# Reordering the head loop of a hybrid decoder kernel: output maps, state products and memory chunks at other places

## The reference, cut to what matters

```python
_, _, h_r, h_i = lax.associative_scan(_cplx_combine, (a_r, a_i, bu_r, bu_i), axis=1)   # 16 groups of 64 states
y = (jnp.einsum('bsgp,gcp->bsgc', h_r, c_re) - jnp.einsum('bsgp,gcp->bsgc', h_i, c_im) + d * ug)
...
s = (jnp.einsum('bqhd,bkhd->bhqk', qn, k_nope) + jnp.einsum('bqhr,bkr->bhqk', qr, k_rope)) * scale
p = softmax32(jnp.where(kpos[None, :] <= t[:, None], s, NEG_INF))                      # 6 heads, and twice 6 of the sparse group
...
kv = (rmsnorm(mem, g_mem) @ wkv).reshape(bsz, m, 2, XATTN_HEADS, XATTN_DIM)            # keys of the memory: four chunks
```

## Time and profile before

| | |
|---|---|
| median of 3 runs | 1681.85 us (1680.43 to 1685.18) |
| profiled execution | 1679.73 us, span 1677.9 us, clock 0.991 |
| VectorE busy | 1338.6 us (80%) |
| ScalarE busy | 1091.2 us (65%) |
| GpSimd busy | 229.7 us (14%) |

### The profile page before, as it was taken

One profiled execution on the slowest core, in us unless ns is written; L12 is line 12 of the kernel. 1 busy time (PEld: TensorE's weight loads), 2 busy tenths in 40 slices (PEclk: granted clock), 3 DMA queues, 4 the chain that ended last, 5 costly groups with the idle time before them and its releaser, 6 DMA issues.

```text
span 1677.9 us, 24224 instructions
## 1 busy us (share of the span) xinstructions
PE 1632.3 (97%) x8466; PEld 1371.8 (82%) x8466; DVE 1338.6 (80%) x1471; ACT 1091.2 (65%) x1231; POOL 229.7 (14%) x240
## 2 busy tenths in 40 slices
PE   8899999999998999999999999999999999999997
PEld 8788888888897888778888888888888888888785
DVE  7986666555668765688988988988989889889897
ACT  7545444445555554467777777777777777777775
POOL 7751001006414300320000000000000000000200
PEclk9999999999999999999999999999999999999998
DMA  9413437755430253399999999999999999999994
GB/s 392 185 51 126 157 120 312 275 179 195 168 138 30 82 181 111 138 411 377 365 379 388 372 382 375 387 380 374 381 369 383 386 375 362 385 375 362 411 384 168
DMA packets 68357, 476.95 MB, mean 284 GB/s; under 512 B 8027, under 2 KB 8161, under 8 KB 13508
## 3 DMA queue, kind: packets, MB, share of 16 engines
q1 hardware_dynamic: 62188, 451.43, 70.2%
q0 software_dynamic: 5584, 22.97, 3.5%
q10 hardware_dynamic: 520, 1.69, 0.3%
HBM read 463.98 MB, written 13.25 MB: 284 GB/s over the span
## 4 chain that ended last, share of the span: by engine, by line
PE 76%; DVE 9%; issue 8%; ACT 3%; POOL 2%; DMA 1%; DVEq 0%; POOLq 0%; SPq 0%; ACTq 0%
PE bank L480 23%; PE bank L482 23%; PE bank L481 23%; DVE lower L504 2%; PE bank L692 1%; DVE lp L2081 1%; ACT upper L523 1%; ACT upper L500 1%; DVE xel L1096 1%; DMA ring<-in_weights 1%; PE bank L1689 1%; DVE row L2081 1%; POOL lp L2555 1%; POOL lp L1250 1%; POOL small L2555 0%
## 5 line engine op out<-in xcount | busy, mean ns | idle before, releaser
L529 DVE TENSOR_TENSOR lower<-ring,upper 128x2048 fp32r<-128x2048 f32 x368 | 847.0, 2302 | 145.3 <-ACT upper L523 132.2
L523 ACT ACTIVATE upper<-ring 128x2048 fp32r<-128x2048 f32 x369 | 706.6, 1915 | 116.7 <-PE bank L482 104.6
L480 PE MATMUL bank<-upper,xeu 128*128 128x512 f32 x896 | 359.8, 402 | 2.1 <-DVE lower L529 1.5
L482 PE MATMUL bank<-upper,xel 128*128 128x512 f32 x896 | 350.5, 391 | 0.0
L481 PE MATMUL bank<-lower,xeu 128*128 128x512 f32 x896 | 349.5, 390 | 0.0
L480 PE MATMUL bank<-upper,htu 128*128 128x512 f32 x536 | 209.7, 391 | 3.5 <-DVE htl L1112 3.5
L482 PE MATMUL bank<-upper,htl 128*128 128x512 f32 x536 | 208.8, 389 | 0.0
L481 PE MATMUL bank<-lower,htu 128*128 128x512 f32 x536 | 208.6, 389 | 0.0
L482 PEld LDWEIGHTS bank<-upper,xel 128*128 128x128 f32 x896 | 168.2, 188 | 35.9
L480 PEld LDWEIGHTS bank<-upper,xeu 128*128 128x128 f32 x896 | 168.3, 188 | 34.9 <-DVE lower L529 2.8
L481 PEld LDWEIGHTS bank<-lower,xeu 128*128 128x128 f32 x896 | 168.7, 188 | 31.7
(11 more groups left out here) (421 smaller groups left out, 2605.7 us busy)
## 6 DMA issues: line engine op xcount, KB each, us to landing
ring<-in_weights SPq DMA_DIRECT2D x422, 1024.0 KB, 6.3
routed_rows<-g POOLq DMA_DIRECT2D x1, 4096.0 KB, 36.7
lp<-in_lparams POOLq DMA_DIRECT2D x1, 3602.5 KB, 14.1
memraw<-routed_rows POOLq DMA_DIRECT2D x7, 512.0 KB, 8.5
expert_rows<-xk POOLq DMA_DIRECT2D x7, 512.0 KB, 7.5
lp<-in_lparams SPq DMA_DIRECT2D x1, 3552.0 KB, 21.0
attn<-in_first SPq DMA_DIRECT2D x2, 1024.0 KB, 6.6
skewed_bias<-bias_rows POOLq DMA_DIRECT2D x1, 1152.0 KB, 27.7
```

The source lines that it names most:

```text
L480: pe.matmul(to, x_up, w_up, start=start, stop=False, skip_group_check=True)
L482: return pe.matmul(to, x_lo, w_up, start=False, stop=stop, skip_group_check=True)
L523: act.activation(upper[:, third(q), :], ring[:, q % RING, :], ACT.Copy).then_inc(done, 1)
L529: dve.tensor_tensor(lower[:, q % RING, :], ring[:, q % RING, :], f32(upper[:, third(q), :]), ALU.subtract).then_inc(done, 1)
```

## The change

It alters only when things are done. On VectorE the output maps move behind the compressed keys and values, where `states(2)` was; `states(2)` moves to step 1; the split of the memory columns moves behind the mask of head 3 (step 0) and that of chunk 7 behind the mask of head 4 (step 1). On TensorE `bu2` moves to step 1 and the first state outputs to the end of step 1. The memory keys move from steps 2, 6, 10, 14 to 3, 7, 11, 14, and the states and their outputs follow the new tables.

```diff
-               ("vm1", "act"), ("kcv", "dve"), ("bu2", "dve"), ("qT0", "act"), ...
+               ("vm1", "act"), ("kcv", "dve"), ("qT0", "act"), ...
-MEMK = {2: 0, 6: 1, 10: 2, 14: 3}
-STATES = {1: 3, 3: 4, 5: 5, 7: 6, 9: 7}
-STATES_OUT = {4: (2, 3), 8: (4, 5), 13: (6, 7)}
+MEMK = {3: 0, 7: 1, 11: 2, 14: 3}
+STATES = {1: 2, 3: 3, 5: 4, 7: 5, 9: 6, 10: 7}
+STATES_OUT = {1: (0, 1), 5: (2, 3), 9: (4, 5), 13: (6, 7)}
...
                 def state_outputs(pair):
+                    if pair[0] == 0:
+                        pe.wait_ge(ct_ready[l], 1)
                     pe.wait_ge(state_ready[l], pair[-1] + 1)
...
-                state_inputs(2)
...
-                pe.wait_ge(ct_ready[l], 1)
-                state_outputs((0, 1))
...
+                def output_maps():
+                    ...
-                states(2)
+                output_maps()
...
-                memory_lower()
...
-                layer_chunk_lower(dve, l, MEM_FIRST)
                 for i in range(HEADS):
                     for n in scored_at(i):
                         masked_scores(n)
+                    if i == 0:
+                        memory_lower()
+                    if i == 1:
+                        layer_chunk_lower(dve, l, MEM_FIRST)
                     if i in MEMK:
                         layer_chunk_lower(dve, l, MEM_FIRST + MEMK[i] + 1)
```

More of the change, by code:

```diff
@@ L101 @@
                ("qn1", "act"), ("bu1", "dve"), ("kn0", "act"), ("kn1", "act"), ("vm0", "act"),
-               ("vm1", "act"), ("kcv", "dve"), ("bu2", "dve"), ("qT0", "act"), ("qT1", "act"), ("qT2", "act"), ("sc", "dve"),
+               ("vm1", "act"), ("kcv", "dve"), ("qT0", "act"), ("qT1", "act"), ("qT2", "act"), ("sc", "dve"),
                ("s0", "dve"), ("s1", "dve"), ("pcT", "act"), ("s2", "dve"), ("oc0", "dve"), ("oc1", "dve")):
@@ L2239, in _ @@
                 dve.wait_ge(lp_landed, 16)
[L2240 to L2248, removed]
+                def output_maps():
+                    frb, fib = (f.unsqueeze(2).broadcast_to([P, 8, 32]) for f in (fr, fi))
+                    t0 = pt[:, 0, 0:256].rearrange("p (j n) -> p j n", j=8)
+                    t1 = pt[:, 1, 0:256].rearrange("p (j n) -> p j n", j=8)
+                    tt(cp[:, 0], ct[:, 0], frb, ALU.mult)
+                    tt(t0, ct[:, 1], fib, ALU.mult)
+                    tt(cp[:, 1], ct[:, 0], fib, ALU.mult)
+                    link(tt(t1, ct[:, 1], frb, ALU.mult))
+                    tt(cp[:, 0], cp[:, 0], t0, ALU.subtract)
+                    dve.scalar_tensor_tensor(cp[:, 1], cp[:, 1], -1.0, t1, ALU.mult, ALU.subtract).then_inc(ct_ready[l], 1)
                 def states(j):
```

## The result

The changed kernel takes 1721.75 us (median of 4 runs, 1720.75 to 1723.49) against 1681.64 us of the kernel before (4 runs, 1680.43 to 1685.18). The ratio is 1.0236, 95% interval 1.0218 to 1.0254: slower by 40 us. The forecast was 1724 us, 1706 to 1740.

A forecast was written before the change was run, and what follows sets the result against it. TensorE, busy 97% of the span, was taken to bound the kernel. Waits and moved work less the old stall and its slow clock gave +26.6 us, new slow clock 17, stated as +43: 1724 us, range 1706 to 1740.

The forecast's parts named there:

- What bounds the kernel: Whole kernel: TensorE, busy 97% of the span, sets the end; reordering can move only idle time, clock and contention.
- 37.8 - 6.2: Both head loops: 37.8 us of new waits and moved work, less 6.2 for the stall of `s5`, before any clock.
- `s5`: Head loops: masking `s3` before the splits removes a 3.08 us wait per layer and its slow clock, 11.2 us together.
- `s6`: Step 3: the pair `s6`, `s7` waits 2.1 us per layer for VectorE to free the bank of `bu2`.
- Before the loop: Six maps replace `states(2)` (4.6 us) and take 4.6 to 5.5 us beside GpSimd; net nothing, bounds -1 and +0.8.
- The chain to the state outputs: From `pT3` through mask, split, states and GpSimd takes 11.1 us against 4.9 of TensorE work: 6.2 us wait, later repeated.
- the first group's two waits: Steps 3 to 5: 6.2 us, some 1.9 at `bu4` and 4.3 before the state outputs of states 2 and 3.
- the second's: Steps 7 to 9: the same chain from `pT7` to the outputs of states 4 and 5, 6.2 us.
- outputs(12): Steps 11 to 13: waits 3.1 us for VectorE's `group_outputs(1)`, where 0.67 stood: +2.4 per layer.
- The clock: Slow clock behind four waits per layer: 2.5 us for each of three, 1 behind `pcT`; 17 us in all, bounds 0 and 33.
- "The clock stays up": Rival for both head loops: the waits come but the clock does not fall, +26.6 us, 1708 us; 14%.
- "Faster": Rival: 11.2 us go, 4.0 of moved work come, `states(3)` and `states(5)` are done in time: 1675 us; 6%.

The follow-up runs named there:

- experiment 7: The changed kernel with matmuls whose results nothing reads put ahead of those that wait, filling TensorE's waits: 1705.67 us, 1.0143 to the kernel before.
- experiment 10: The kernel before with matmuls whose results nothing reads, 6 before the first state outputs and 12 before `s5`: 1676.67 us, 0.9971.
- experiment 5: The kernel before with only the memory columns' split moved to step 0 and chunk 7's split kept in step 1: 1682.28 us, 1.0006.
- Experiment 2: The changed kernel with the second and third group of state outputs in steps 7 and 11 instead of 5 and 9: 1705.21 us, 1.0143 to the kernel before.
- experiment 1: The changed kernel with the memory keys back in steps 2, 6, 10, 14: 1712.44 us, 1.0183 to the kernel before.
- 3: The changed kernel with the output maps back ahead of `states(0)` and nothing in their place: 1714.43 us, 1.0190 to the kernel before.
- experiment 8: The kernel before with state 2 moved into the loop, later states and outputs rescheduled, splits behind the masks, maps and chunks unmoved: 1680.50 us, 0.9999.
- 9: The kernel of experiment 8 with `bu3` ahead of step 2's memory product and `states(3)` ahead of the split: 1676.11 us, 0.9973 to the kernel before.

## Why the prediction was right

- **What bounds the kernel.** Right: the instructions of TensorE stayed, and the 41 us are idle time, moved work and clock. Experiments 7 and 10 give 30.0 us for waits and moved work, where the forecast has 37.8 - 6.2 = 31.6, and 11.9 for the clock, where it has 17 - 5.0 = 12.0. (Its sum, 26.6 + 17 = 43.6, gives 1725 rather than 1724; that changes nothing.)
- **`s5`.** Its wait went, as said. That 11.2 us went with it holds only because the chunk behind it moved to step 3 as well: experiment 5 shows that with the chunk in step 2 the wait passes to it, at 2.78 us. In the changed kernel the same debt is paid at `s6` (2.37 us, forecast 2.1).
- **Before the loop.** Right. The six maps took 4.7 us (523.64 to 528.38) for a forecast of 4.6 to 5.5. TensorE idles 3.31 us before `pcT` (forecast 3.9), and `pcT` comes 10.35 us after `kn1`, 10.66 before. Three of the four products, with GpSimd at work beside them, and the first of the last two, without it:

```profile
524.46 1.48 DVE L2080 TENSOR_TENSOR pt<-lp,small 128x256 f32<-128x256 f32 x1
525.86 0.94 DVE L2080 TENSOR_TENSOR cp<-lp,small 128x256 f32<-128x256 f32 x1
526.73 0.94 DVE L2080 TENSOR_TENSOR pt<-lp,small 128x256 f32<-128x256 f32 x1
527.70 0.42 DVE L2080 TENSOR_TENSOR cp<-cp,pt 128x256 f32<-128x256 f32 x1
```

  Six at 0.42 would be 2.5 us, so it was right to reckon with GpSimd. Each of the four products ends 0.2 to 0.3 us after an operation of GpSimd ends (524.25, 525.65, some 526.5 and 527.39 in its timeline), as the forecast had it. The rule of the Trainium skill, "SBUF — State Buffer", section "SBUF: two separate sides", that such operations of the two engines exclude each other, fits the difference.
- **The chain to the state outputs.** Right in mechanism and in length (11.2 us for 11.1). Experiment 2 took the waits for GpSimd away by asking later, with no change to the chain. In layer 1 the first group's two waits sum to 6.2 us, as forecast, the second's to 4.8; in layer 0 they are 4.65 and 4.74. So three of the four were forecast some 1.5 us too long. In layer 1 the missing 1.4 us are in TensorE's own work between: from the start of `bu4` to the state outputs and from that of `bu6` it is 6.45 and 6.46 us, of which TensorE works 2.08 us at clock 1.00 in the first and 3.50 us at 0.56 in the second. The chain beside it sets the time, so there the slow clock costs nothing; it only takes the place of a wait. Layer 0 has it in both groups (0.55 behind `bu4`, 0.53 behind `bu6`).
- **outputs(12).** 2.31 us for a forecast of 3.1, so +1.6 a layer, not +2.4: mis-sized by 0.8.
- **The clock.** 17 us forecast for the waits of the changed kernel, 16 measured by experiment 7. The total is partly luck, since errors cancel: the forecast charged nothing behind the wait of 2.1 us (the clock lost 1.7 there in layer 1, nothing in layer 0), and a mean of 2.5 behind the other three, where layer 1 shows 4.2, 2.1 and 1.7 and layer 0 3.4, 1.7 and 1.7. Behind `pcT` it charged 1, since VectorE is partly the bound there. The windows lose 1.7 in layer 1 and 2.9 in layer 0, but the way from `pcT` to `s6` is 1.25 and 2.33 us longer than in experiment 7, so that is what they cost.
- **The rivals.** "The clock stays up", 1708, falls with the windows, and experiment 7 shows what it would have been: 1706. That the clock would fall was not sure: it rested on two falls behind 3.08 us, and other waits here kept 1.00, see the last section. "Faster" falls: VectorE's mask of `s7` waited 6.66 us for `pT3`, so `states(3)` was not done in time.

What stays open: experiments 1 to 3 gave back 9.3, 16.5 and 7.3 us, 33 of the 40, but the edits aren't independent and no run had all three, so these are no shares of the loss.

## What to carry to other kernels

Before moving work of a slow engine "behind" something, list for each engine the instruction that frees the buffer which its next one needs: here a memory chunk of 5.84 us between two small products held up a mask, and with it three engines. Leave the whole length of a chain over several engines between its start and the step that asks for its result. And count a wait of the bounding engine with the clock behind it: here that added 12 us to the 30 of waits and moved work.

## What was unexpected of the hardware

- **The same wait does not always bring the low clock.** Behind an idle of 1.60 us the granted clock was 1.00 in the kernel before and 0.57 over 510 to 514 us in experiment 5; behind 0.92 us it was 0.57 in experiment 8 and 1.00 in 9; behind 1.8 us 1.00 (556.4) and 0.56 (581.1) in one profile. Idles of 3 us and more in these head loops, 3.08 to 4.37, were followed by about half clock in every place of the changed kernel and the one before. In experiment 1 the fall came late: behind an idle of 4.08 us the state outputs still ran at full speed (1.11 us at 578.07), and only some 1 us after the restart did the products take 0.41 us and not 0.28. The level of 0.50 is 1.2 GHz, that of 1.00 is 2.4.
- **A wait need not be filled to its end.** In experiment 7 the 12 matmuls left 1.62 us of idle before the state outputs, and the clock behind it stayed at 1.00:

```profile
552.12 1.06 PE L1483 MATMUL bank<-lp,cp 128*32 128x256 f32 x8 [1.62 <-POOLq L2645]
```

- **A gain at the start is lost to GpSimd.** ScalarE's copy of the rotated keys in layer 0 waits for GpSimd's table. In six of the thirteen profiled executions TensorE was 2 us ahead here (ScalarE's copy of the values starts at 53.4 to 54.2 us, not 55.3 to 57.0), and waited 1.7 to 3.5 us for that table a few us later, as in experiment 10:

```profile
63.12 4.47 PE L1522 MATMUL bank<-lp,ql 128*128 128x384 f32 x8 [3.45 <-ACT attn L1906]
```

  That copy starts at 59.5 to 61.9 us in all thirteen, so the 2 us are lost again; in the six it starts at 60.5 us or later.
